# Layer-1 attention of a streaming encoder: batches in groups of three row tiles, one projection slice a batch, first scores inside the last input unit

## The reference, cut to what matters

```python
z = h @ w_in + b_in
q, k, v = jnp.split(z, [C_HEADS * C_DH, C_HEADS * C_DH + C_KV * C_DH], axis=-1)
q, k = rope(q, pos), rope(k, pos)
s = jnp.einsum('...qkgd,...jkd->...kgqj', q, k) * (C_DH ** -0.5)
p = jax.nn.softmax(jnp.concatenate([s, sink], axis=-1), axis=-1)[..., :-1]
o = jnp.einsum('...kgqj,...jkd->...qkgd', p, v)
return h + o @ w_out
```

## Time and profile before

| | |
|---|---|
| median of 3 runs | 2465.24 us (2463.98 to 2466.7) |
| profiled execution | 2467.93 us, its span 2466.1 us |
| PE, DVE, ACT, POOL busy | 97%, 57%, 33%, 9% of the span |
| mean granted TensorE clock | 0.986 of full speed |

### The profile page before, as it was taken

One profiled execution on the slowest core, in us unless ns is written; L12 is line 12 of the kernel. 1 busy time (PEld: TensorE's weight loads), 2 busy tenths in 40 slices (PEclk: granted clock), 3 DMA queues, 4 the chain that ended last, 5 costly groups with the idle time before them and its releaser, 6 DMA issues.

```text
span 2466.1 us, 36673 instructions
## 1 busy us (share of the span) xinstructions
PE 2391.8 (97%) x15073; PEld 2303.7 (93%) x15073; DVE 1401.9 (57%) x1976; ACT 815.1 (33%) x1465; POOL 218.5 (9%) x147
## 2 busy tenths in 40 slices
PE   8998898999999999999999989999999999999998
PEld 7998677999999999999999957899999999999998
DVE  4445665665555655555574576566555556555557
ACT  5323566432222222222144475333222222222214
POOL 3435001000000000000040043200000000000003
PEclk9999999999999999999999989999999999999999
DMA  5112100211111111111002100021111111111101
GB/s 154 53 52 73 32 14 10 69 52 52 51 51 34 34 51 34 51 51 49 19 2 72 45 10 14 14 86 52 35 51 51 51 34 34 51 34 51 51 1 74
DMA packets 108162, 110.97 MB, mean 45 GB/s; under 512 B 3320, under 2 KB 97951, under 8 KB 108076
## 3 DMA queue, kind: packets, MB, share of 16 engines
q1 hardware_dynamic: 103140, 107.30, 13.8%
q10 hardware_dynamic: 4936, 2.47, 0.4%
HBM read 99.92 MB, written 9.42 MB: 44 GB/s over the span
## 4 chain that ended last, share of the span: by engine, by line
PE 90%; DVE 4%; ACT 3%; POOL 1%; issue 1%; DMA 0%; ACTq 0%; DVEq 0%; POOLq 0%
PE PS L234 76%; PE PS L2435 2%; PE PS L2026 2%; PE PS L369 2%; PE PS L2417 1%; PE PS L2060 1%; PE PS L2372 1%; PE PS L2216 1%; PE PS L2044 1%; PE PS L2388 1%; PE PS L2267 1%; DVE nm L1438 1%; PE PS L2393 1%; ACT zs_e L841 1%; PE PS L1957 0%
## 5 line engine op out<-in xcount | busy, mean ns | idle before, releaser
L234 PE MATMUL PS<-xhi,uphi_f 128*128 128x364 f32 x2064 | 457.5, 330 | 0.9 <-issue 0.9
L234 PE MATMUL PS<-xlo,uphi_f 128*128 128x364 f32 x2064 | 456.0, 330 | 0.0
L234 PE MATMUL PS<-xhi,uplo_f 128*128 128x364 f32 x2064 | 455.8, 329 | 0.0
L234 PEld LDWEIGHTS PS<-xhi,uphi_f 128*128 128x128 f32 x2064 | 358.2, 188 | 2.4 <-issue 1.5
L234 PEld LDWEIGHTS PS<-xlo,uphi_f 128*128 128x128 f32 x2064 | 358.7, 188 | 0.0
L234 PEld LDWEIGHTS PS<-xhi,uplo_f 128*128 128x128 f32 x2064 | 358.4, 188 | 0.0
L1642 DVE TENSOR_TENSOR resid<-PS,resid 128x728 f32<-128x728 f32 x320 | 216.7, 719 | 181.8 <-PE PS L234 181.8
L234 PE MATMUL PS<-hhi_f,dhi_f 128*128 128x364 f32 (+1 forms) x1008 | 223.2, 330 | 2.2 <-DVE hlo_f L1313 2.2
L234 PE MATMUL PS<-hlo_f,dhi_f 128*128 128x364 f32 (+1 forms) x1008 | 222.8, 330 | 0.0
L234 PE MATMUL PS<-hhi_f,dlo_f 128*128 128x364 f32 (+1 forms) x1008 | 222.8, 330 | 0.0
L1041 ACT COPY edge<-ext_f 128x4 f32 (+1 forms) x86 | 17.1, 198 | 532.0 <-DVE ext_f L1568 532.0
(11 more groups left out here) (315 smaller groups left out, 3422.5 us busy)
## 6 DMA issues: line engine op xcount, KB each, us to landing
graw<-in_w_up SPq DMA_DIRECT2D x22, 1024.0 KB, 5.1
vraw<-in_w_up SPq DMA_DIRECT2D x22, 1024.0 KB, 5.1
draw<-in_w_down SPq DMA_DIRECT2D x22, 1024.0 KB, 4.9
wraw<-in_w_in_even SPq DMA_DIRECT2D x16, 512.0 KB, 3.9
wraw<-in_w_in_odd SPq DMA_DIRECT2D x10, 512.0 KB, 4.3
out_y_prompt<-yN SPq DMA_DIRECT2D x8, 512.0 KB, 2.7
xnat<-in_x_prompt SPq DMA_DIRECT2D x3, 1024.0 KB, 6.2
out_diff_k_prompt<-kNat ACTq DMA_DIRECT2D x4, 512.0 KB, 3.4
```

Source lines behind the costliest of these rows:

```text
L234: last = nc.tensor.matmul(PS[:, 3 * s + c, 0:width], w, x[:, a:a + width], start=(k == 0 and n == 0), stop=(k == nk - 1 and n == 2))
```

## The change

Batches are reordered: three groups of three row tiles, in each first b=2 and then b=3, and behind them b=0 and b=1 over all tiles as before. So the rows of the first row chunk are complete after six batches. Slices now go by row chunk, all eight units in the first chunk, then in the second, then in the third; one slice a step in steps 10 to 29, then in 32, 35, 36 and 37; steps 30, 31, 33 and 34 have none. A unit's weights are therefore loaded and split three times. Outputs go to bank 7 only for batches 1, 3 and 5, all others to bank 6. Input units 2 to 9 now make the query tiles 4, 5, 6, 7, 0, 1, 2, 3, so that b=2 and b=3 are ready first and unit 9 is needed by b=1 only. The scores of batch 0 move into the last input unit, behind its fifth of eight product groups, and DVE runs `odd_max(0)` ahead of the eviction of that unit. `last_rope` moves to steps 5 to 7. The loops over units are written out.

```diff
-        BATCHES = [(t, b) for b in (2, 3, 0, 1) for t in range(RT)]
+        BATCHES = [(t, b) for g in range(3) for b in (2, 3) for t in range(3 * g, 3 * g + 3)] + [(t, b) for b in (0, 1) for t in range(RT)]
...
-        FO_K = 4
-        FO_START = 22
-        FO_AT = {FO_START + 2 * n + i: [[3 * n + 2 * i], [3 * n + 1] if i == 0 else []] for n in range(8) for i in range(2)}
...
+        FO = 3 * KT
+        FO_STEPS = list(range(10, 30)) + [32, 35, 36, 37]
+        FO_AT = {q: j for j, q in enumerate(FO_STEPS)}
+        FO_READY = {8: 0}
+        FO_READY.update({FO_STEPS[j] - 1: j for j in range(1, FO)})
+        SWAP9 = {1: 0, 2: 1, 3: 2, 4: 3}
+        ROPE9 = {5: 0, 6: 1, 7: 2}
+
+        def query_tile(u):
+            return (u + 2) % KT
...
-            return 7 if q % 2 and q < 2 * RT // FO_GROUPS else 6
+            return 7 if q % 2 and q < 6 else 6
...
-                    for w in range(FO_UNITS):
+                    for j in range(FO):
...
-            for s in range(2):
-                odd_queries(8 + s, s, False)
+            for u in range(2, 8):
+                odd_queries(u, u % 2, True)
+            odd_queries(8, 0, False)
+            odd_max(0)
+            odd_queries(9, 1, False)
...
             for q in range(STEPS):
...
                 if q >= 4 and q in FO_AT:
                     odd_out_lo(q - 4)
-                if q < NQ:
+                if 1 <= q < NQ:
                     odd_max(q)
                 if q >= 4 and q not in FO_AT:
                     odd_out_lo(q - 4)
                 if 1 <= q <= NQ:
                     odd_den(q - 1)
-                for j in slots[0]:
-                    fo_add(j)
+                if q in FO_READY:
+                    fo_lo(FO_READY[q])
+                if q in FO_AT:
+                    fo_add(FO_AT[q])
                 if 2 <= q < NQ + 2:
                     odd_probs_rest(q - 2)
...
-                    reached(pe, 1, "in_rope", 2 * b + 3)
+                    reached(pe, 1, "in_rope", 2 * ((b + 2) % 4) + 3)
...
+            def first_scores(k):
+
+                if k == 4:
+                    reached(pe, 1, "in_ev", 9)
+                    odd_scores(0)
+
+            for u in range(4, 10):
+                odd_unit(u, u % 2, u - 1, first_scores if u == 9 else None)
...
             for q in range(STEPS):
-                if q < NQ:
+                if 1 <= q < NQ:
                     odd_scores(q)
-                slots = FO_AT.get(q, [[], []])
-                for j in slots[0]:
-                    fo_products(j)
+                if q in FO_AT:
+                    fo_products(FO_AT[q])
```

More of the change, by code:

```diff
@@ L603, in _ @@
             sp.dma_start(kc2n[:, :], io["cache_swa_k"][0, 0].rearrange("s g d -> s (g d)")).then_inc(S("kc_in"), 16)
-            with sp.Fori(1, 5) as j:
-                for s in range(2):
-                    col = sp.snap(j * 256 + (s - 2) * P)
-                    reached(sp, 1, "in_lo", 2 * j + s - 1)
-                    sp.dma_start(wraw[:, s], src[:, :, bass.ds(col, P)]).then_inc(S(f"in_raw{s}"), 16)
+            for u in range(2, 10):
+                col = query_tile(u) * P
+                reached(sp, 1, "in_lo", u - 1)
+                sp.dma_start(wraw[:, u % 2], src[:, :, col:col + P]).then_inc(S(f"in_raw{u % 2}"), 16)
             sp.wait_ge(S("oi_kn"), 2)
@@ L1144, in last_swap @@
                 a = 32 * (c ^ 1)
-                last = identity(zs_o[32 * c:32 * c + 32, :], z_o[a:a + 32, :], bias=par[a:a + 32, 6, P_BIN + 7:P_BIN + 8])
+                last = identity(zs_o[32 * c:32 * c + 32, :], z_o[a:a + 32, :], bias=par[a:a + 32, 6, P_BIN + query_tile(9):P_BIN + query_tile(9) + 1])
                 if c == 3:
@@ L1151, in swap_bias @@
                 ropes = u - 1 if not isinstance(u, int) or u else 0
-                row = u - 2 + P_BIN if not isinstance(u, int) or u else P_BIN + 8
+                row = query_tile(u) + P_BIN if u else P_BIN + 8
                 reached(act, 1, "in_ev", u + 1)
@@ L1194, in _ @@
             value_rows(2, 8, 1, DEC)
[L1195 to L1198, removed]
+            for u in range(4, 8):
+                odd_hi(u + 2, u % 2)
+                swap_bias(u)
             swap_bias(8)
@@ L1813, in last_rope @@
             def last_rope(n):
-                b = par[:, 6, P_BIN + 7:P_BIN + 8]
+                k = query_tile(9)
+                b = par[:, 6, P_BIN + k:P_BIN + k + 1]
                 if n == 0:
@@ L1823, in last_rope @@
                     reached(dve, 1, "in_rz", 9)
-                    tt(q2T[:, 7, :], z_o[:, :], zs_o[:, :], ALU.add).then_inc(S("in_rope"), 1)
+                    tt(q2T[:, k, :], z_o[:, :], zs_o[:, :], ALU.add).then_inc(S("in_rope"), 1)
             for q in range(STEPS):
-                slots = FO_AT.get(q, [[], []])
-                for j in FO_AT.get(q - 1, [[], []])[1]:
-                    fo_add(j)
                 if q >= 4 and q in FO_AT:
                     odd_out_lo(q - 4)
-                if q < NQ:
+                if 1 <= q < NQ:
                     odd_max(q)
@@ L1837, in _ @@
                     odd_den(q - 1)
-                for j in slots[0]:
-                    fo_add(j)
+                if q in FO_READY:
+                    fo_lo(FO_READY[q])
+                if q in FO_AT:
+                    fo_add(FO_AT[q])
                 if 2 <= q < NQ + 2:
                     odd_probs_rest(q - 2)
[L1842 to L1845, removed]
+                if q in ROPE9:
+                    last_rope(ROPE9[q])
                 if q in (NQ - 4, NQ - 2):
@@ L2348, in _ @@
                 last.then_inc(S("oi_vtr"), 1)
-            with pe.Fori(2, 5) as j:
-                for s in range(2):
-                    odd_unit(2 * j + s, s, 2 * j + s - 1)
             def odd_scores(q):
@@ L2421, in fo_products @@
             def fo_products(j):
-                w, c = j // 3, j % 3
+                c = j // KT
                 a, width = CHUNKS[c]
[L2425 to L2428, removed]
+                reached(pe, 1, "pq_lo", j + 1)
+                if j % KT == 0:
+                    pe.wait_ge(S("om_lo"), 6 * c + 6)
                 if j:
                     reached(pe, 1, "pq_ev", j)
-                for n in range(FO_K):
-                    k = HK + FO_K * (w // KT) + n
-                    x = [xn1[i][:, k, a:a + width] for i in range(2)]
+                for n in range(HK):
+                    x = [xn1[i][:, HK + n, a:a + width] for i in range(2)]
                     for m, (wt, y) in enumerate(((fohi, x[0]), (fohi, x[1]), (folo, x[0]))):
-                        last = nc.tensor.matmul(PS[:, 7, 0:width], wt[:, w % 2, n, :], y,
-                                                start=(n == 0 and m == 0), stop=(n == FO_K - 1 and m == 2))
+                        last = nc.tensor.matmul(PS[:, 7, 0:width], wt[:, j % 2, n, :], y,
+                                                start=(n == 0 and m == 0), stop=(n == HK - 1 and m == 2))
                 last.then_inc(S("pq_mm"), 1)
+            def first_scores(k):
[4 more added lines that the diff above has]
+                odd_unit(u, u % 2, u - 1, first_scores if u == 9 else None)
             pe.wait_ge(S("oi_vn"), 3)
@@ L2453, in _ @@
                     odd_probs(q - 2)
-                for j in slots[1]:
-                    fo_products(j)
             out_projection(OUTP[1])
```

27 lines of the change are left out of this document (9 added, 18 removed).

## The result

The changed kernel takes 2476.42 us (median of 20 runs, 2465.71 to 2483.47); the kernel before 2468.57 (20 runs, the earlier three among them, 2463.98 to 2472.92). The ratio is 1.0027, 95% interval 1.0016 to 1.0038: **slower by 7.9 us**. The forecast was 2467.4 with a range to 2473.0, so the result lies outside. The median needs one remark: 13 of the 20 runs have a mean granted clock of 0.981 to 0.984 and take 2476.2 us or more, seven have 0.986 to 0.989 and take 2465.7 to 2470.4. The profiled execution, 2477.96 us with a span of 2476.1, is one of the 13.

The account below looks back on a forecast made before the run. PE, busy 97% of the span, was taken as the bound, so only its idle time and lower clock could move. -5.3 - 5.5 + 0.6 + 7.4 + 5.0 = +2.2 on 2465.24 gave 2467.4 us, range 2458.5 to 2473.

Parts of the forecast that it names:

- batch 10's scores earlier: Stage start to batch 10's scores: these begin 5.3 us earlier, 2.3 up to batch 5's scores and 3.0 behind.
- slices cover pauses, less the full batch at the cut: From batch 10 on: one slice a step saves 5.5 us; a full batch behind the cut adds 0.6.
- four pauses: Steps 30, 31, 33, 34: values wait for bank 6, so PE idles 1.85 us each, 7.4 more.
- the clock in these pauses: Behind the pauses of steps 30 to 34: three clock falls of four, 5.0 us more, bounds 0 and 10.
- slower rival: Steps 30 to 35: clock falls at 30 and stays down through slices, 5 us above forecast, 2472.4; chance 0.19.
- A step without a slice at 5.0: Steps 30, 31, 33, 34: each costs 5.0 us with its pause, nearly as one with a slice.
- The first probabilities 2.8 earlier: Stage start: first scores inside unit 9 let the first probabilities start at 1419.8 instead of 1422.60, 2.8 us earlier.
- Slices hidden behind PE: Steps from 10 on: the slices' work on ACT and DVE and added weight loads hide behind PE's 5.2 us.
- Batch 5's scores: Stage start: ACT reaches step 4 2.3 us earlier, so these scores start at 1431.0 instead of 1433.28; bounds 0.5 and 2.9.
- The five steps behind it: Batch 5's to batch 10's scores: 19.3 us instead of 22.3, including 3.5 for rotary work and its clock risk.
- the wait of 2.48 for the rotary work: Before batch 10's scores: PE's 2.48 us wait for unit 9's rotary result goes, as only b=1 needs it.

Follow-up runs that it names:

- e2: Changed kernel with ten products nobody reads put between scores and values in steps 30, 31, 33 and 34: 2465.95 us.
- e8: Changed kernel with ten products nobody reads between scores and values in steps 33 and 34 only: 2469.64 us.
- e1: Changed kernel with DVE running the low part of the output ahead of the maximum in every step from 10 on: 2464.54 us.
- e4: Changed kernel with slices moved to steps 14 to 37 (2456.79 us), and the first scores and maximum put back into step 0: 2461.56 us.
- e5: Changed kernel with slices moved to steps 14 to 37 (2456.79 us), and both halves of each slice's weight split done twice: 2473.71 us.
- e6: Changed kernel with slices in steps 14 to 37 (2456.79 us), last rotary work in steps 6, 8, 10, slices' readiness wait at step 13: 2456.30 us.
- b1: Kernel before with only the order of query tiles changed to 4 to 7, then 0 to 3: 2466.48 us, ratio 0.9992.

## Why the prediction failed, by its own steps

Lengths in the stage, of the profile of after against that of before; batch 10's scores are counted from unit 8's eviction (54.70 before, 49.17 after). The second line is what is left of the 9.3.

| step | forecast | measured |
|---|---|---|
| batch 10's scores earlier | -5.3 | -5.5 |
| slices cover pauses, less the full batch at the cut | -4.9 | -4.8 |
| four pauses | +7.4 | +7.9 |
| the clock in these pauses | +5.0 | +11.7 |
| sum | +2.2 | +9.3 |

**The step that failed is "The clock in these pauses".** It took three falls of 3.3 us at 0.50 each, with 10 as its upper bound. What came was two stretches of 13.6 and 13.7 us, in which PE was busy 11.70 and 11.78; at full speed that work takes half, so they cost 11.7. e2 measured the same by itself: 12.0 by the medians, 10.8 in the stage. The slower rival had the mechanism, a clock that stays down from one pause through the next into the slices of steps 32 and 35; its 20 us of work at half clock were 23.5, and its 2472.4 lay 4.0 too low, for a second reason as well. Before's median was 2465.24 in three runs and is 2468.57 in 20; that is 3.3 of the 9.0 us by which 2467.4 missed. As a difference, +2.2 stands against +7.9, and 6.7 of the profile's miss are this step.

Where the argument went wrong: it priced a fall at 3.3 us, what followed 0.43 and 0.82 of pause, the shortest fall of the stage. Nearer rows were in its own list. The pause of 2.48, in one piece like the new ones, lies in a window of 12.83 us with a mean clock of 0.74, which is 6.7 us at 0.50 (0.26 of 12.83, times two). Four falls at that price are 26.7 us, and 27.3 came. The start of the stage, named in the slower rival, had some 13.5 us at 0.50, behind pauses of 4.30 and 0.93; the first of them in PE's timeline before:

```profile
1420.12 1.56 PE L2372 MATMUL PS<-kd,q2T 64*64 64x192 f32 x16 [4.30 <-ACT E L1212]
```

Whether each of the four pauses brings its own 6.8 us or two of them together 13.6, no run tells: none leaves one pause of a pair by itself.

The rule of the Trainium skill, page "TensorE: Matmul & The Clock Gate", section "HAM oscillation — how this bites in real kernels", which puts the fall down to single gaps longer than these, would have had the term at 0. The trace disagrees: the clock fell behind pauses of 1.77 to 2.32 us, and e2 and e8 show that filling those pauses, and nothing else, keeps it up. The prediction was right to go by the row against the rule, and went too short a way.

**What was right.** The pauses: forecast 1.85 each, measured 1.77, 1.90, 2.32 and 1.90, ended by `xlo` as named, and e1 shows that the order on DVE makes them. A step without a slice at 5.0: with the clock held (e2) the five steps took 25.05, for four times 5.0 and one of 5.2. The first probabilities 2.8 earlier: 3.0 (e4). Slices hidden behind PE: yes at their size, with room that e5 used up.

**Right in the sum, not in the parts.** Batch 5's scores came 3.9 earlier than before (counted from unit 8's eviction: 32.39 and 28.53), for a forecast of 2.3, which kept the start's 13.5 us at 0.50; there were 6.8 (0.16 of 21.14, times two). The five steps behind it took 20.64 for a forecast of 19.3. Their pauses were put down to the rotary work; e6 moved that work and they stayed (5.3 and 5.4). That the wait of 2.48 for the rotary work "goes" was too simple: b1, which takes away just this wait, gains 0.2 us in the stage.

**Left open:** why some runs of the changed kernel keep a mean clock of 0.986 and more. The time follows the clock, but no profile caught such a run, so whether one fall is missing there or both was not seen. That these runs lie around the forecast of 2467.4 does not bear it out. The runs of e2, whose profile has no fall behind step 30, spread over 10.1 us as well (2459.74 to 2469.84).

## What to carry to other kernels

Where one engine is full over nearly the whole span, count pauses of 2 us among small products as more than their length: here 7.9 us of pauses cost 11.7 more through the granted clock, and the repair that gave most was to spread work that was there anyway (one slice a step to the end) over the steps that had none. Price a fall of the clock by the stretch of the trace whose pauses look most like the new ones, in length and in number, and not by the shortest fall in it. And when a wait is taken away, ask what the same steps wait for next; where ScalarE's and VectorE's chain is as late as the wait that went, nothing is gained.

## What the runs showed of the hardware that was not expected

- Two pauses of 1.8 to 2.3 us, some 7 us apart, brought 13.6 us at 0.50, five times in three profiles (twice each in the two of the changed kernel, once in e8), always 13.6 or 13.7 long; pauses of 0.6 to 1.4 us in the same places (e1) left the clock at 1.00. The length behind other pauses varied: at the start of the stage 2.84 and some 0.45 of pause were followed by 6.8 us at 0.50 in the changed kernel and by 3.4 in e6.
- The same split on DVE took 0.66 us in the changed kernel, and 1.26 (once, before) and 1.84 (the second of two in a row, e5) beside POOL's operation, behind whose end it ended by 0.55. Why was not tested.
